# Expert gates of a product-key layer: a table built by adding transfers in main memory, in place of one-hot products on TensorE

## The chip, the cores and the metric

One core of a Trainium2 chip. The metric is the device time of the program in microseconds (us), the median of several executions. The compared kernels run the same inference step on the same inputs.

## What is computed

One decoder layer for 256 prompt tokens and 8 sample tokens (T = 264 columns in all) of width 2048. After the two attention branches comes the part that the change touches, a layer of 16384 experts of which each token takes 16 per head, in 8 heads:

```python
def peer_route(h, w_q, sub_keys):
    q = (h @ w_q).reshape(T, PEER_HEADS, 2, PEER_DK)
    s = jnp.einsum('thpd,hpkd->thpk', q, sub_keys).astype(jnp.float32)
    sv, si = lax.top_k(s, PEER_TOPK)
    cand = (sv[:, :, 0, :, None] + sv[:, :, 1, None, :]).reshape(T, PEER_HEADS, PEER_TOPK * PEER_TOPK)
    cv, ci = lax.top_k(cand, PEER_TOPK)
    ia = jnp.take_along_axis(si[:, :, 0], ci // PEER_TOPK, axis=-1)
    ib = jnp.take_along_axis(si[:, :, 1], ci % PEER_TOPK, axis=-1)
    return ia * N_KEYS + ib, jax.nn.softmax(cv, axis=-1)
...
        act = jax.nn.gelu(jnp.einsum('td,thkd->thk', hi, eu[ii]).astype(jnp.float32), approximate=False)
        return jnp.einsum('thk,thkd->td', (act * gi).astype(hi.dtype), ev[ii])
```

Expert number = 128 ia + ib. Nearly every expert is wanted by some token, so the kernel computes all 16384 x 264 scores densely, takes their gelu, multiplies by a dense table of gates (0 where a token did not choose the expert; the sum of the gates where several heads chose it), and multiplies the result by the dense matrix of expert outputs.

## The kernel before, in words

**Units of weights.** All large products run as "units". A unit is one load of 1 MB (128 x 2048 float32) into a ring of four slots (`RING`, `wr`, issued by SP in `load_w` after `wait_slot`), which ACT rounds to a high part (`high_part`, L420) and DVE completes by a low part (`low_part`, L425), each in four quarters; TensorE then makes three products of every 128 x 128 block (`products`, L577 to L579), 48 matmuls of 264 columns per unit. High and low parts have room for one unit, so a quarter is prepared while TensorE works through the other three quarters of the unit before. Units follow each other in one order (`STREAM`) on SP, ACT, DVE and PE.

**The expert layer** has 128 score units (`peer_u`, one unit for each value of ia: 128 experts) and 128 output units (`peer_v`; four units, a "group", for each four values of ia). The activations of 64 values of ia fill the buffer `ACTS`, so the layer runs in two halves:

1. 64 score units "u0". Between their quarters DVE runs the routing (`routing()`: three passes for 128, 128 and 8 tokens; top-16 of the keys, top-16 of the pairs, softmax), and PE turns the resulting lists so that tokens lie in columns (`turn_results`).
2. `weights(0)`: 66 jobs that make the gates of the first 64 values of ia. For each eight tokens DVE writes two one-hot matrices of the chosen ia (`OHA`, L1928) and ib (`OHB`, L1930), GpSimd multiplies the first by the gates (L1448), PE multiplies them token by token (L1065), and DVE multiplies the activations by the product, read from PSUM (`weigh`, L2083). No unit runs in this stage.
3. A loop `for it in 0..7` that alternates an output group of the first half with four score units of the second half ("vu"), whose activations take the place of those just used.
4. `weights(1)`, as 2.
5. 64 output units ("v1"). In an output group ACT and DVE split the weighted activations (L1341, L2091) and DVE adds the products to x (`add_outputs`, L2101).

Then comes the last normalisation `norm(2)` and the embedding part ("ple"), whose weights `wple` and `pT` GpSimd loads when the expert layer is over (L1456, L1457).

Of the kernel before, what the change touches and what calls it, by code (L numbers as in the profile page):

```python
# [23 lines left out]
P = 128  # L24
# [4 lines left out]
NH = 8  # L29
# [17 lines left out]
STREAM = [("A", 56), ("gates", 32), ("up", 16), ("out", 16), ("wq", 16), ("u0", 64), ("vu", 128), ("v1", 64), ("ple", 16)]  # L47
# [19 lines left out]
for _u in range(32):  # L67
    JOB_LIST += [(f"gate{_u}", 1)] + SLOT.get(_u, [])
JOB_LIST += [("up", 16), ("out", 16),
            ("norm1", 1), ("wq", 16), ("key", 9), ("u0", 64), ("wb0", 66), ("u1", 64), ("wb1", 66), ("norm2", 1), ("ple", 16)]  # L70
JOB = {}
SPLIT_JOBS = ("A", "out", "wq", "u0", "u1", "ple") + tuple(f"gate{_u}" for _u in range(32))
# [15 lines left out]
def stream_of(n):  # L88

    for name, s in (("A", S0["A"]), *((f"gate{u}", S0["gates"] + u) for u in range(32)), ("out", S0["out"]),  # L90
                    ("wq", S0["wq"]), ("u0", S0["u0"]), ("ple", S0["ple"])):
# [11 lines left out]
EXPS, TURN = (19, 43, 51), (28, 52, 56)  # L103
# [5 lines left out]
C_EPS, C_EPS128, C_SEL, C_RT, C_OWNH, C_FOLD, C_END = 1984, 1985, 1986, 2017, 2023, 2027, 2035  # L109


def constants():
# [24 lines left out]
    for half in range(2):  # L137
        for parity in range(2):
            for g in range(4):
                row = 32 * (2 * half + parity) + g  # L140
                c[row, C_OWNH + g] = 1
                c[row, C_FOLD + 4 * half + g] = 1
    c[:, C_EPS] = EPS
# [8 lines left out]
def build(nc, xT, pT, wd, vd, wsmall, wple, subk, kx, vx, lx, state, convst, params, consts, ptab,  # L152
          o_x, o_k, o_v, o_lf, o_sp, o_ss, o_cs):
    with ExitStack() as ctx:
# [100 lines left out]
        ACTS = BIG  # L255
        IDX = CST + C_INV
        assert IDX + 3 * T <= CST + C_CAUS
        OHA = ACTS + HALF * T
        OHB = OHA + 2 * 8 * HALF
        assert OHB + 2 * 8 * P <= NF  # L260

# [19 lines left out]

        FIRST_ON = tuple((a - ACTS) // T for a in (SCORE[0], SCORE[1], RS2))
# [75 lines left out]
        turned, idx_ready, al_ready = sem("turned"), sem("idx_ready"), sem("al_ready")  # L358
# [106 lines left out]
        def _(sp):  # L465
# [71 lines left out]
            loop(S0["u0"], 136, 16)  # L537
            with sp.Fori(0, 16) as it:
                for kind in range(2):
                    for j in range(RING):  # L540
                        s = S0["vu"] + 4 * kind + j
                        wait_slot(sp, it, 8, s, RING)
                        load_w(it, 4, s, (vd, wd)[kind], (j, 200 + j)[kind])
            loop(S0["v1"], 64, 16, vd)
# [15 lines left out]
        def _(pe):  # L560
# [471 lines left out]
            def turn_results(c):  # L1032
                pe.wait_ge(res_ready, c + 1)
                for i in range(3):
                    if c == 2:
                        last = mm(ps[:, 6, i * P:i * P + NS], at(LX + i * P, P, 64), at(ROW_T, NS, 64), start=True, stop=True)
                    else:
                        last = nc.tensor.transpose(ps[:, 4 + c, i * P:(i + 1) * P], at(RES[c] + i * P, P), ident)
                last.then_inc(turned, 1)

            for c in range(3):
                key_scores(c)

            done = 0
            for c in range(4):
                upto = (TURN + (64,))[c] // 4
                with pe.Fori(done, upto) as it:
                    for j in range(RING):
                        split_unit(it, 4, S0["u0"] + j, JOB["u0"] + j)
                done = upto  # L1050
                if c < 3:
                    turn_results(c)

            def weights(half):
                wb = JOB[f"wb{half}"]

                def weights_of(it, j):
                    pe.wait_ge(oha_ready, it * 4 + (33 * half + j + 1))
                    pe.wait_ge(ohb_ready, it * 4 + (33 * half + j + 1))
                    for n in (wb + 2 * j, wb + 2 * j + 1):  # L1060
                        pe.wait_ge(evac[n % 4], it * 2 + n // 4)
                        for i in range(4):
                            t = 4 * (n - wb - 2 * j) + i
                            oha = at(OHA + (j % 2) * 8 * HALF + t * HALF, HALF)
                            last = mm(bank(n)[:, i * P:(i + 1) * P].rearrange("p (r a) -> p r a", a=HALF),  # L1065
                                      at(OHB + (j % 2) * 8 * P + t * P, P),
                                      oha.unsqueeze(1).broadcast_to([P, 2, HALF]), start=True, stop=True)
                        last.then_inc(pe_job, 1)

                with pe.Fori(0, 8) as it:  # L1070
                    for j in range(4):
                        weights_of(it, j)
                weights_of(8, 0)

            def outputs(it, m, s, g, buf):

                pe.wait_ge(al_ready, it * 2 + (g + 1))
                for dq in range(RING):
                    for q in range(RING):
                        pe.wait_ge(y_added, it * 32 + (16 * g + 4 * dq + q + 1))  # L1080
                        wait_low_part(pe, it, m, s + dq, q)
                        for j in range(EG):
                            a = (buf * EG + j) * T
# [5 lines left out]
            weights(0)  # L1089
            pe.wait_ge(idx_ready, 3)  # L1090
            with pe.Fori(0, 8) as it:
                for b in range(2):
                    outputs(it, 16, S0["vu"] + 8 * b, b, b)
                    for j in range(RING):
                        split_unit(it, 16, S0["vu"] + 8 * b + 4 + j, JOB["u1"] + 4 * b + j, 8)
            weights(1)
            with pe.Fori(0, 8) as it:
                for b in range(2):
                    outputs(it, 8, S0["v1"] + 4 * b, 16 + b, b)
# [15 lines left out]
        def _(act):  # L1115
# [190 lines left out]
            def high_only(name):  # L1306

                dense_steps(act, S0[name], 4, high_part, lambda it, j: None)
# [3 lines left out]
            each_block("wq", 4, ACT.Copy, QT, final=False)  # L1312
# [6 lines left out]

            for u in range(64):  # L1320
                for q in range(RING):
                    high_part(act, 0, 0, S0["u0"] + u + 1, q)
                wait_quarter(act, 0, 0, S0["u0"] + u, RING - 1)
                if u in FIRST_ON:
                    act.wait_ge(res_ready, FIRST_ON.index(u) + 1)
                n = JOB["u0"] + u
                A(at(ACTS + u * T, T), bank(n)[:, 0:T], ACT.Gelu).then_inc(evac[n % 4], 1)
                if u in EXPS:
# [3 lines left out]
                    gates = at(RES[c] + 2 * P, 16 * heads, m)  # L1332
                    A(gates, gates, ACT.Exp).then_inc(re_exp, 1)

            def slots(a, n, it, m):
                a = ACTS + a * T
                return at(a + it * m * T, n * T) if isinstance(it, int) else arena[:, bass.ds(it * (m * T) + a, n * T)]

            def high_of_group(it, g, buf):
                rows = at(ACTS, HALF * T).rearrange("p (a t) -> p a t", t=T)[:, bass.ds(it * 8 + 4 * g, EG), :]  # L1340
                A(rd_(AH + buf * EG * T, EG * T).rearrange("p (a t) -> p a t", t=T), rows, ACT.Copy).then_inc(ah_ready, 1)  # L1341

            def value_parts(it, m, s, b, last, nothing_after=False):
                for j in range(RING):
                    for q in range(RING):
                        if not (nothing_after and last and j == RING - 1):
                            high_part(act, it, m, s + j + 1, q)
                    if j == 1 and not (last and b == 1):

                        high_of_group(it, b + 1, 1 - b)  # L1350

            def both(it, last=False):
                for b in range(2):
                    s = S0["vu"] + 8 * b
                    value_parts(it, 16, s, b, last)
                    for j in range(RING):
                        for q in range(RING):
                            high_part(act, it, 16, s + 5 + j, q)
                        wait_quarter(act, it, 16, s + 4 + j, RING - 1)
                        n = JOB["u1"] + 4 * b + j  # L1360
                        if j == 0:
                            act.wait_ge(al_ready, it * 2 + (b + 1))
                        A(slots(4 * b + j, 1, it, 8), bank(n)[:, 0:T], ACT.Gelu).then_inc(evac[n % 4], 1)
# [3 lines left out]
            for half in range(2):  # L1367
                for b in range(4):
                    wait_evac(act, JOB[f"wb{half}"] + 62 + b)
                high_of_group(0, 0, 0)  # L1370
                if half == 0:
                    with act.Fori(0, 7) as it:
# [866 lines left out]
```

## Time and profile before

| | us |
|---|---|
| median of 3 runs | 3101.51 (3099.52 to 3107.52) |
| the profiled execution | 3104.63 |
| its span in the profile | 3103.0 |
| PE busy | 2945.5 (95%) |
| DVE busy | 1918.7 (62%) |
| ACT busy | 1228.9 (40%) |
| POOL (GpSimd) busy | 201.6 (6%) |
| main memory traffic | 519.60 MB, mean 167 GB/s |

The profiled execution took 3.1 us more than the median of the runs; its span is 1.6 us shorter than its own time. Busy times of engines overlap, so the shares tell which engine is never long idle (PE), and the stages have to be looked at one by one to see what each costs.

### The profile page before, as it was taken

To read this page: it belongs to the slowest core of one execution; us is meant where nothing else is said; L and a number is where in the kernel's file an instruction comes from. 1 tells how busy PE (TensorE), PEld (TensorE's weight loads), DVE (VectorE), ACT (ScalarE), POOL (GpSimd) and SP (SyncE) were. 2 spreads that over 40 slices of the span, in tenths; PEclk is the share of its full clock that TensorE was granted. 3 is DMA by queue.
4 is the path that set the end of the run, shared out by engine and by line. 5 is a ranking of instruction groups with operands and counts; after the bars stand their busy time and mean duration, and the time that the engine had idled before them with its cause. 6 is when DMAs were issued, how large, how long until landed. Compare 5 with 4: busy or idle time off the path is not lost.

```text
span 3103.0 us, 60917 instructions
## 1 busy us (share of the span) xinstructions
PE 2945.5 (95%) x23119; PEld 2804.4 (90%) x23119; DVE 1918.7 (62%) x3707; ACT 1228.9 (40%) x2123; POOL 201.6 (6%) x227
## 2 busy tenths in 40 slices
PE   6999999989999998999998799999999978999999
PEld 6999868877878898999997799999999978999989
DVE  4467446545442345588868856656656687777764
ACT  4455421033330244445551144444444412444454
POOL 2100011000000000000004300000000042000000
PEclk8999979989899998999999999999999999999999
DMA  5545335547564444445542154454455512444543
GB/s 189 188 177 180 131 117 188 190 172 297 218 255 164 152 161 153 157 177 179 187 176 82 46 185 176 181 184 176 181 184 176 182 62 73 184 176 178 185 154 123
DMA packets 83934, 519.60 MB, mean 167 GB/s; under 512 B 11170, under 2 KB 11442, under 8 KB 30834
## 3 DMA queue, kind: packets, MB, share of 16 engines
q1 hardware_dynamic: 74882, 488.03, 43.4%
q0 software_dynamic: 7792, 25.95, 2.2%
q10 hardware_dynamic: 1152, 4.19, 0.4%
q8 instruction: 65, 1.06, 0.1%
q14 instruction: 43, 0.35, 0.0%
HBM read 508.75 MB, written 9.39 MB: 167 GB/s over the span
## 4 chain that ended last, share of the span: by engine, by line
PE 90%; DVE 6%; issue 2%; DMA 1%; ACT 0%; DVEq 0%; POOL 0%; POOLq 0%; SPq 0%; ACTq 0%
PE ps L577 25%; PE ps L578 25%; PE ps L579 24%; PE ps L1001 4%; PE ps L811 2%; DVE arena L1930 1%; DVE arena L2083 1%; DVE arena L1928 1%; PE ps L897 1%; PE ps L653 1%; PE ps L637 1%; PE ps L798 1%; PE ps L572 1%; DVE arena L1474 1%; PE ps L934 1%
## 5 line engine op out<-in xcount | busy, mean ns | idle before, releaser
L425 DVE TENSOR_TENSOR split<-arena,split 128x512 fp32r<-128x512 f32 x1568 | 1080.8, 692 | 840.2 <-ACT split L420 833.7
L420 ACT ACTIVATE split<-arena 128x512 fp32r<-128x512 f32 x1568 | 987.5, 631 | 1267.8 <-PE ps L579 1267.3
L577 PE MATMUL ps<-split 128*128 128x264 f32 x4224 | 1216.5, 288 | 45.2 <-DVE split L425 41.5
L578 PE MATMUL ps<-split 128*128 128x264 f32 x4224 | 1206.0, 286 | 0.0
L579 PE MATMUL ps<-split 128*128 128x264 f32 x4224 | 1205.1, 285 | 0.0
L577 PEld LDWEIGHTS ps<-split 128*128 128x128 f32 x4224 | 805.4, 191 | 71.1 <-DVE split L425 35.6
L578 PEld LDWEIGHTS ps<-split 128*128 128x128 f32 x4224 | 806.0, 191 | 0.5
L579 PEld LDWEIGHTS ps<-split 128*128 128x128 f32 x4224 | 801.5, 190 | 0.0
L577 PE MATMUL ps<-rounded,split 128*128 128x264 f32 x2048 | 584.1, 285 | 10.7 <-DVE rounded L2091 10.7
L578 PE MATMUL ps<-rounded,split 128*128 128x264 f32 x2048 | 584.4, 285 | 0.0
L579 PE MATMUL ps<-rounded,split 128*128 128x264 f32 x2048 | 580.6, 283 | 0.0
L577 PEld LDWEIGHTS ps<-rounded,split 128*128 128x128 f32 x2048 | 387.1, 189 | 11.1 <-issue 11.1
L578 PEld LDWEIGHTS ps<-rounded,split 128*128 128x128 f32 x2048 | 386.8, 189 | 0.0
L579 PEld LDWEIGHTS ps<-rounded,split 128*128 128x128 f32 x2048 | 386.3, 189 | 0.0
L2101 DVE TENSOR_TENSOR arena<-arena,ps 128x264 f32<-128x264 f32 x512 | 216.4, 423 | 0.0
L1448 POOL TENSOR_TENSOR arena<-arena 128x512 f32<-128x512 f32 x66 | 122.7, 1860 | 1290.2 <-DVE arena L1928 1290.2
L1065 PE MATMUL ps<-arena 128*128 128x128 f32 x1056 | 134.5, 278 | 47.6 <-POOL arena L1448 47.6
L1065 PEld LDWEIGHTS ps<-arena 128*128 128x128 f32 x1056 | 122.7, 189 | 59.3 <-issue 36.9
L1001 PE MATMUL ps<-arena 128*128 128x264 f32 x512 | 117.2, 391 | 0.7 <-DVE arena L1874 0.7
L1001 PEld LDWEIGHTS ps<-arena 128*128 128x128 f32 x512 | 98.6, 193 | 19.0 <-issue 0.8
L1341 ACT ACTIVATE rounded<-arena 128x1056 fp32r (+1 forms) x32 | 34.3, 1073 | 181.4 <-DVE arena L2083 181.4
L1930 DVE TENSOR_TENSOR arena<-arena 128x1024 f32<-128x1024 f32 x66 | 80.4, 1218 | 0.0
(323 smaller groups left out, 1702.3 us busy)
## 6 DMA issues: line engine op xcount, KB each, us to landing
arena<-in_wd SPq DMA_DIRECT2D x280, 1024.0 KB, 4.8
arena<-in_vd SPq DMA_DIRECT2D x128, 1024.0 KB, 4.8
arena<-in_kx SPq DMA_DIRECT2D x64, 512.0 KB, 4.6
arena<-in_vx SPq DMA_DIRECT2D x32, 512.0 KB, 6.7
arena<-in_vx POOLq DMA_DIRECT2D x32, 512.0 KB, 6.8
early<-in_state SPq DMA_DIRECT2D x8, 512.0 KB, 9.6
o_ss<-early ACTq DMA_DIRECT2D x8, 512.0 KB, 9.1
arena<-in_xT SPq DMA_DIRECT2D x1, 2112.0 KB, 8.6
```

The source lines that it names most:

```text
L420: nc.scalar.activation(ckh(q), at(WR + (s % 4) * D_MODEL + q * QW, QW), ACT.Copy).then_inc(hi_ready, 1)
L425: nc.vector.tensor_tensor(ckl(q), at(WR + (s % 4) * D_MODEL + q * QW, QW), as_f32(ckh(q)), ALU.subtract).then_inc(lo_ready, 1)
L577: mm(out, wh, xh, start=start, stop=False)
L578: mm(out, wh, xl, start=False, stop=False)
L579: return mm(out, wl, xh, start=False, stop=stop)
L811: last = mm(bank(n)[:, i * P:(i + 1) * P], at(lhs + o, P), at(rhs + o, P), start=True, stop=True)
L1001: last = mm(ps[:, n % 4 + 4 * half, 0:T], wr(j)[:, (half * NH + k) * P:(half * NH + k + 1) * P], ot3[:, half * NH + k, :], start=(k == 0), ...
L1065: last = mm(bank(n)[:, i * P:(i + 1) * P].rearrange("p (r a) -> p r a", a=HALF), at(OHB + (j % 2) * 8 * P + t * P, P), oha.unsqueeze(1).br ...
L1341: A(rd_(AH + buf * EG * T, EG * T).rearrange("p (a t) -> p a t", t=T), rows, ACT.Copy).then_inc(ah_ready, 1)
L1448: nc.gpsimd.tensor_tensor(oh, oh, gate, ALU.mult).then_inc(oha_ready, 1)
L1930: V.tensor_tensor(at(OHB + (j % 2) * 8 * P, 8 * P).rearrange("p (t b) -> p t b", b=P), cst(C_IOTA).unsqueeze(1).broadcast_to([P, 8, P]), a ...
L2101: V.tensor_tensor(xt3[:, d, :], xt3[:, d, :], ps[:, 4 + q, 0:T], ALU.add).then_inc(y_added, 1)
```

## The change

The expert layer is no longer halved. The 128 score units run first ("u"), then the 128 output units ("v"). The activations go to a table `acts` in main memory: ACT writes the gelu of a unit to a ring of 16 in the arena (`ACTR`), and SP stores each four of them. The gates are a table `gates` of 128 x 128 x 264 floats in main memory. ACT's queue clears it by 32 transfers during the units "out" and "wq" (`clear_gates`). The routing now ends in element numbers (`LIN`), and GpSimd issues 384 indirect transfers (3 passes x 8 heads x 16 choices), each of which adds one gate of each token to its element of the table; after each 16 it waits until all have landed, since two heads may choose the same expert. For each output group SP loads the group's activations and gates (`load_activations`), GpSimd multiplies them, ACT and DVE split the product. `weights`, `onehots`, `weigh`, `gate_rows` and two of three `turn_results` are gone.

```diff
-STREAM = [("A", 56), ("gates", 32), ("up", 16), ("out", 16), ("wq", 16), ("u0", 64), ("vu", 128), ("v1", 64), ("ple", 16)]
+STREAM = [("A", 56), ("gates", 32), ("up", 16), ("out", 16), ("wq", 16), ("u", 128), ("v", 128), ("ple", 16)]
...
+        gates = nc.dram_tensor("gates", (N_KEYS, P, T), F32, kind="Internal").ap()
+        acts = nc.dram_tensor("acts", (N_KEYS // EG, P, EG * T), F32, kind="Internal").ap()
+        gate_rows = gates.rearrange("a b (t o) -> (a b t) o", o=1)
+        GRP = EG * T
...
+            def store_activations(g):
+                n = JOB["u"] + 4 * g + 3
+                wait_evac(sp, n)
+                sp.dma_start(acts[g], at(ACTR + (g % 4) * GRP, GRP)).then_inc(act_stored, 16)
+
+            def load_activations(g):
+
+                if g >= 2:
+                    sp.wait_ge(al_ready, g - 1)
+                else:
+                    sp.wait_ge(gates_added, 16 * 3 * P)
+                sp.wait_ge(act_stored, 16 * (g + 1))
+                w = gates[4 * g:4 * g + 4].rearrange("a b t -> b a t")
+                sp.dma_start(at(ABUF + g % 2 * GRP, GRP), acts[g]).then_inc(aw_loaded[g % 2], 16)
+                sp.dma_start(at(WBUF + g % 2 * GRP, GRP).rearrange("p (a t) -> p a t", t=T), w).then_inc(aw_loaded[g % 2], 16)
+
+            peel(S0["u"], 136, wd)
+            for g in range(32):
+
+                for j in range(RING):
+                    s = S0["u"] + 4 * (g + 1) + j
+                    wait_slot(sp, 0, 0, s, RING)
+                    load_w(0, 0, s, *((wd, 136 + 4 * (g + 1) + j) if g < 31 else (vd, j)))
+                if g:
+                    store_activations(g - 1)
+            load_activations(0)
+            load_activations(1)
+            store_activations(31)
+            for g in range(32):
+                if g < 31:
+                    for j in range(RING):
+                        s = S0["v"] + 4 * (g + 1) + j
+                        wait_slot(sp, 0, 0, s, RING)
+                        load_w(0, 0, s, vd, 4 * (g + 1) + j)
+                if g < 30:
+                    load_activations(g + 2)
...
-            weights(0)
-            pe.wait_ge(idx_ready, 3)
-            with pe.Fori(0, 8) as it:
+            pe.wait_ge(rows_read, 1)
+            with pe.Fori(0, 16) as it:
                 for b in range(2):
-                    outputs(it, 16, S0["vu"] + 8 * b, b, b)
-                    for j in range(RING):
-                        split_unit(it, 16, S0["vu"] + 8 * b + 4 + j, JOB["u1"] + 4 * b + j, 8)
-            weights(1)
-            with pe.Fori(0, 8) as it:
-                for b in range(2):
-                    outputs(it, 8, S0["v1"] + 4 * b, 16 + b, b)
+                    outputs(it, b)
...
+            def clear_gates(it, a):
+
+                dst = gates.rearrange("(g a) b t -> g b a t", a=EG)
+                dst = dst[it * 4 + a // 4] if isinstance(it, int) else dst[bass.ds(it * 4 + a // 4, 1)].rearrange("o b a t -> (o b) a t")
+                act.dma_start(dst, at(ZT, T).unsqueeze(1).broadcast_to([P, EG, T])).then_inc(gates_zero, 16)
...
+            def high_of_group(it, b):
+                act.wait_ge(prod_ready, it * 2 + (b + 1))
+                A(rd_(AH + b * GRP, GRP), at(ABUF + b * GRP, GRP), ACT.Copy).then_inc(ah_ready, 1)
...
-            for half in range(2):
-                def gate_rows(it, j):
-                    pool.wait_ge(oh_step, it * 4 + (33 * half + j + 1))
-                    oh = at(OHA + (j % 2) * 8 * HALF, 8 * HALF).rearrange("p (t a) -> p t a", a=HALF)
-                    gate = arena[:, bass.ds(it * 32 + (IDX + 2 * T + 8 * j), 8)].unsqueeze(2).broadcast_to([P, 8, HALF])
-                    nc.gpsimd.tensor_tensor(oh, oh, gate, ALU.mult).then_inc(oha_ready, 1)
...
-            pool.wait_ge(y_added, 516)
+            pool.wait_ge(gates_zero, 16 * N_KEYS // EG)
+            for c in range(3):
+                pool.wait_ge(lin_ready, c + 1)
+                m = P if c < 2 else NS
+                source = RES[c] + 2 * P if c < 2 else RT2 + 2 * P
+                for h in range(NH):
+                    for k in range(16):
+                        e = 16 * h + k
+                        pool.indirect_dma_start(gate_rows, bass.IndirectOffsetOnAxis(at(LIN + c * P + e, 1, m).bitcast(U32), 0),
+                                                at(source + e, 1, m), None, compute_op=ALU.add).then_inc(gates_added, 16)
+                    pool.wait_ge(gates_added, 16 * (P * c + 16 * h + 16))
+
             pool.dma_start(at(WPL, PLE_KT * D_MODEL), wple).then_inc(ple_in, 16)
             pool.dma_start(at(PTI, PLE_KT * T), pT).then_inc(ple_in, 16)
+
+            with pool.Fori(0, 16) as it:
+                for b in range(2):
+                    pool.wait_ge(aw_loaded[b], it * 32 + 32)
+                    a = at(ABUF + b * GRP, GRP)
+                    nc.gpsimd.tensor_tensor(a, a, at(WBUF + b * GRP, GRP), ALU.mult).then_inc(prod_ready, 1)
...
+                    m2, firsts = (m, RE) if c < 2 else (NS, RT2)
+                    row = at(LT, P, m2)
+                    ch(V.tensor_scalar(row, at(firsts, P, m2), float(P * T), cst(C_TOK + c, 1, m2), ALU.mult, ALU.add))
+                    ch(V.scalar_tensor_tensor(out=row, in0=at(firsts + P, P, m2), scalar=float(T), in1=row, op0=ALU.mult, op1=ALU.add))
+                    V.tensor_copy(at(LIN + c * P, P, m2).bitcast(U32), row).then_inc(lin_ready, 1)
```

What the queues hold now, at two places. On GpSimd, behind the load of the sub-keys (`SK`), the kernel before has the multiplications of the one-hot rows and then the loads for "ple":

```order
L1450 ISA
L1448 ISA [waits onehot_step]
L1448 TENSOR_TENSOR arena<-arena 128x512
L1445 REGISTER_ALU
...
L1450 COMPARE_AND_BRANCH
L1448 TENSOR_TENSOR arena<-arena 128x512 [waits onehot_step]
L1456 DMA arena<-in_wple 128x4096 [waits y_added]
L1457 DMA arena<-in_pT 128x528
```

and the changed kernel (L1442 is the adding transfer, L1453 the product of activations and gates; the pair of L1442 rows stands 24 times in all):

```order
L1442 DMA gates<-arena 4325376x1 [waits lin_ready,gates_zero]
L1442 DMA gates<-arena 4325376x1 x15
...
L1442 DMA gates<-arena 4325376x1 [waits gates_added]
L1442 DMA gates<-arena 4325376x1 x15
L1446 DMA arena<-in_wple 128x4096 [waits gates_added]
L1447 DMA arena<-in_pT 128x528
...
L1453 TENSOR_TENSOR arena<-arena 128x1056 [waits aw_loaded0]
L1453 TENSOR_TENSOR arena<-arena 128x1056 [waits aw_loaded1]
```

All 384 adding transfers now stand on GpSimd's queue ahead of the products. On SP, where score units end and output units begin, the changed kernel has (L483 the loads of units, L549 a store of activations, L559 and L560 the loads of a group's activations and gates):

```order
L483 DMA arena<-in_vd 128x2048 [waits lo_ready] x4
L549 DMA acts<-arena 128x1056 [waits evac3]
L559 DMA arena<-acts 128x1056 [waits act_stored,gates_added]
L560 DMA arena<-gates 128x4x264
L559 DMA arena<-acts 128x1056 [waits act_stored,gates_added]
L560 DMA arena<-gates 128x4x264
L549 DMA acts<-arena 128x1056 [waits evac3]
L483 DMA arena<-in_vd 128x2048 [waits lo_ready] x4
L559 DMA arena<-acts 128x1056 [waits act_stored,al_ready]
L560 DMA arena<-gates 128x4x264
```

Before, SP had nothing but loads of units there. The first loads of activations and gates now stand behind the loads of the first four output units, and wait for the last adding transfer.

## Rows read from the trace of the kernel before

**Rows 1.** The page: engines, and the chain that ended last.

```profile
PE 2945.5 (95%) x23119; PEld 2804.4 (90%) x23119; DVE 1918.7 (62%) x3707; ACT 1228.9 (40%) x2123; POOL 201.6 (6%) x227
PE 90%; DVE 6%; issue 2%; DMA 1%; ACT 0%; DVEq 0%; POOL 0%; POOLq 0%; SPq 0%; ACTq 0%
```

**Rows 2.** Windows by stage: u0, weights(0), vu, weights(1), v1.

```profile
core 0: us, PE busy (x) PEld busy (x) DVE busy (x) ACT busy (x) POOL busy (x), PEclk, DMA share, GB/s
1284.00:1656.00 372.00, 372.00 (x3078) 371.80 (x3077) 293.30 (x776) 188.11 (x329) 3.68 (x2) 1.00 0.49 177
1656.00:1756.00 100.00, 68.98 (x541) 62.95 (x540) 96.52 (x135) 2.36 (x4) 61.36 (x33) 0.98 0.04 15
1756.00:2501.00 745.00, 745.00 (x6142) 745.00 (x6141) 456.51 (x782) 353.44 (x589) 0.00 (x0) 1.00 0.50 179
2501.00:2596.00 95.00, 67.74 (x532) 61.74 (x532) 91.00 (x131) 1.99 (x3) 57.70 (x31) 0.99 0.03 11
```

**Rows 3.** Timeline of PE where stages meet (start, duration, instruction).

```profile
1284.04 0.39 PE L577 MATMUL ps<-split 128*128 128x264 f32 x1
...
1656.87 0.28 PE L579 MATMUL ps<-split 128*128 128x264 f32 x1
...
1755.29 0.58 PE L577 MATMUL ps<-rounded,split 128*128 128x264 f32 x1 [7.22 <-DVE rounded L2091]
...
2501.06 0.28 PE L579 MATMUL ps<-split 128*128 128x264 f32 x1
...
2595.69 0.58 PE L577 MATMUL ps<-rounded,split 128*128 128x264 f32 x1 [3.46 <-DVE rounded L2091]
```

**Rows 4.** Timeline of ACT and DVE in an output group of v1.

```profile
2701.92 0.63 ACT L420 ACTIVATE split<-arena 128x512 fp32r<-128x512 f32 x1 [0.82 <-PE ps L579]
...
2703.91 1.07 ACT L1341 ACTIVATE rounded<-arena 128x1056 fp32r x1
...
2702.59 0.69 DVE L425 TENSOR_TENSOR split<-arena,split 128x512 fp32r<-128x512 f32 x1 [0.42 <-ACT split L420]
2703.20 0.42 DVE L2101 TENSOR_TENSOR arena<-arena,ps 128x264 f32<-128x264 f32 x1
...
2705.14 1.26 DVE L2091 TENSOR_TENSOR rounded<-arena,rounded 128x1056 fp32r<-128x1056 f32 x1
```

**Rows 5.** Timeline of PE after the expert layer.

```profile
2983.65 1.16 PE L1108 MATMUL ps<-arena 128*128 128x264 f32 x4 [1.60 <-DMA arena<-in_pT]
```

**Rows 6.** Timeline of DVE: the last steps of the routing's passes.

```profile
1420.84 0.29 DVE L2030 TENSOR_TENSOR arena<-arena 128x128 f32<-128x128 f32 x1
...
1557.48 0.29 DVE L2030 TENSOR_TENSOR arena<-arena 128x128 f32<-128x128 f32 x1
...
1598.12 0.68 DVE L2038 TENSOR_TENSOR arena<-arena 64x128 f32<-64x128 f32 x3
```

**Rows 7.** Instructions of POOL by line and shape: transfers issued, products.

```profile
L1448 POOL TENSOR_TENSOR arena<-arena 128x512 f32<-128x512 f32 x66 | 122.7, 1860 | 1290.2 <-DVE arena L1928 1290.2
L1394 POOL DMA_DIRECT2D early<-in_lx x64 | 31.2, 488 | 26.5 <-issue 26.5
L451 POOL DMA_DIRECT2D arena<-in_vx x32 | 17.0, 530 | 272.2 <-PE ps L897 238.8 <-issue 33.4
L1402 POOL DMA_DIRECT2D o_lf<-arena x1 | 1.0, 1036 | 0.0
```

**Rows 8.** DMA issues: KB each, median us from issue to landing.

```profile
arena<-in_kx SPq DMA_DIRECT2D x64, 512.0 KB, 4.6
early<-in_lx POOLq DMA_DIRECT2D x64, 4.0 KB, 2.9
o_lf<-arena POOLq DMA_DIRECT2D x1, 12.0 KB, 7.0
```

**Rows 9.** Timeline where DVE and POOL collide, end of weights(0).

```profile
1749.51 1.84 POOL L1448 TENSOR_TENSOR arena<-arena 128x512 f32<-128x512 f32 x1 [3.55 <-DVE arena L1928]
...
1750.37 1.53 DVE L1928 TENSOR_TENSOR arena<-arena 128x512 f32<-128x512 f32 x1
```

More of the change, by code:

```diff
@@ L69 @@
 JOB_LIST += [("up", 16), ("out", 16),
-            ("norm1", 1), ("wq", 16), ("key", 9), ("u0", 64), ("wb0", 66), ("u1", 64), ("wb1", 66), ("norm2", 1), ("ple", 16)]
+            ("norm1", 1), ("wq", 16), ("key", 9), ("u", 128), ("norm2", 1), ("ple", 16)]
 JOB = {}
-SPLIT_JOBS = ("A", "out", "wq", "u0", "u1", "ple") + tuple(f"gate{_u}" for _u in range(32))
+SPLIT_JOBS = ("A", "out", "wq", "u", "ple") + tuple(f"gate{_u}" for _u in range(32))
 PJ = []
@@ L1075, in outputs @@
-            def outputs(it, m, s, g, buf):
-                pe.wait_ge(al_ready, it * 2 + (g + 1))
+            with pe.Fori(0, TURN // 4) as it:
+                for j in range(RING):
+                    split_unit(it, 4, S0["u"] + j, JOB["u"] + j)
+            pe.wait_ge(res_ready, 1)
+            for i in range(3):
+                last = mm(ps[0:NS, 6, i * P:(i + 1) * P], at(ROW_T, NS, 64), at(LX + i * P, P, 64), start=True, stop=True)
+            last.then_inc(turned, 1)
+            with pe.Fori(TURN // 4, 32) as it:
+                for j in range(RING):
+                    split_unit(it, 4, S0["u"] + j, JOB["u"] + j)
@@ L1343, in value_parts @@
[L1343 to L1352, printed above, removed]
+                    rows = at(RES[c] + 2 * P, 16 * heads, m)
@@ L1353, in both, with value_parts @@
+                    A(rows, rows, ACT.Exp).then_inc(re_exp, 1)
+            with act.Fori(4, 8) as it:
+                for u in range(16):
+                    gelu(it, u)
+            def high_of_group(it, b):
+                act.wait_ge(prod_ready, it * 2 + (b + 1))
+                A(rd_(AH + b * GRP, GRP), at(ABUF + b * GRP, GRP), ACT.Copy).then_inc(ah_ready, 1)
+            def value_parts(it, last=False):
                 for b in range(2):
-                    s = S0["vu"] + 8 * b
-                    value_parts(it, 16, s, b, last)
@@ L1365, in _ @@
+                        if j == 1 and not (last and b == 1):
+                            high_of_group(it, b + 1) if b == 0 else high_of_group(it + 1, 0)
             for j in range(4):
                 act.wait_ge(state_saved[j], 32)
-            for half in range(2):
[L1368 to L1372, printed above, removed]
-                        both(it)
-                    both(7, True)
-                else:
-                    with act.Fori(0, 7) as it:
-                        for b in range(2):
-                            value_parts(it, 8, S0["v1"] + 4 * b, b, False)
-                    for b in range(2):
-                        value_parts(7, 8, S0["v1"] + 4 * b, b, True)
+            high_of_group(0, 0)
@@ L1382, in _ @@
+            with act.Fori(0, 15) as it:
+                value_parts(it)
+            value_parts(15, True)
             norm(2)
@@ L2137, in _ @@
+            low_of_group(0, 0)
+            with dve.Fori(0, 15) as it:
+                add_outputs(it)
+            add_outputs(15, True)
             dve.wait_ge(y_added, 516)
```

228 lines of the change are left out of this document (65 added, 163 removed).

## The prediction

> **What bounds the kernel now.** I read the page first, then a table of windows with one row for each stage of the expert layer, then PE's timeline at the seams, then the queues of GpSimd. The page says that PE is busy 95% of the span and that 90% of the chain that ended last is PE's [rows 1]; the reader should see that only a stage without PE work, or a wait of PE, can be worth anything. The windows show where such a stage is. In u0 and vu PE is busy every microsecond (372.00 of 372, 745.00 of 745) at full clock, and DMA engines are busy half the time. In weights(0) and weights(1) DVE is the full one (96.5 of 100, 91.0 of 95), PE has 68 us of small products, and DMA is almost idle, 0.04 and 0.03 [rows 2]. So two stages of the expert layer are bound by DVE and build only the gate table.
>
> PE's timeline gives their exact price. The last product of u0 starts at 1656.87 and the first of vu at 1755.29: 98.4 us. The same pair around weights(1) is 2501.06 and 2595.69: 94.6 us. Together 193.0 us [rows 3]. It also gives the pace of a unit: u0 is 64 units from 1284.04 to 1656.99, 5.83 us each, and vu is 128 units in 745 us, 5.82 us each. Score units and output units cost the same, and mixing them is free.
>
> **What is removed.** Both weight stages, 193.0 us of PE's time line, all of it on the path. The 256 units stay: 256 x 5.83 us whichever way they are ordered, so the reordering costs nothing. The ends of the stages (7.2 us and 3.5 us of PE's wait for DVE's first low part of activations [rows 3]) lie inside the 193.0. The two dropped turns of results are six small products, below 1 us; I take 0.
>
> **What is added at the one seam that is left.** In the changed order SP issues the first loads of activations and gates only behind the fourth output unit's load, which waits for the low part of the last score unit. That low part comes 1.4 us after a quarter of PE ends (ACT 0.63, DVE 0.69, and 0.1 of hops [rows 4]), one unit ahead, so 5.83 - 1.4 = 4.4 us before PE ends its score units. A 512 KB load lands 4.6 us after its issue [rows 8]; here a unit of 1 MB and a store stand in front of two such loads, and I take 6.5 us (bounds 4.6 and 3 x 4.6 = 13.8). Then GpSimd's product of 1056 elements, ACT's 1.07 and DVE's 1.26 [rows 4] follow in series. GpSimd took 1.86 us for 512 elements [rows 7]. But of that 1.84 us at 1749.51 it stood beside a DVE instruction until about 1750.4 and ended at 1751.35 [rows 9], which leaves 0.95 us for 512, or 2.0 us for 1056; the upper bound is 1.86 x 1056 / 512 = 3.8. Sum: -4.4 + 6.5 + 2.0 + 1.07 + 1.26 + 0.5 for hops = 7 us of PE idle (bounds 5 and 16). I take 7.
>
> **What becomes cheaper at the end.** `wple` and `pT` are loaded before the output units, so PE's wait of 1.60 us for `pT` [rows 5] goes: 1.6 us.
>
> **The output units with GpSimd beside them.** DVE's L1928 took 1.53 us in place of 0.69 where it met a GpSimd product [rows 9]: an instruction of DVE that reads two tensors of SBUF waits until GpSimd is done. Every group gets one product of 2.0 to 3.8 us, so one low part of the group may come that much late. A low part is ready 1.4 us after its quarter ends and is needed three quarters later, 3 x 1.46 = 4.4 us: 3.0 us of slack, which hides 2.0 us whole. At 3.8 us the excess is 0.8 us, with the add behind it (0.42) 1.2 us, 32 times: 39 us. DVE has the time, since four units need 16 x (0.61 + 0.42) + 1.26 = 18 us (0.61 is L425 less the overlap with what follows it, 2703.20 - 2702.59 [rows 4]) and a group lasts 23.3 us. I take 0; bounds 0 and 39.
>
> **Transfers that hide.** The table of gates and the activations are 17.3 MB each, written and read once: 69 MB more. A unit is 1 MB in 5.83 us at a DMA share of 0.49 [rows 2]. Clearing adds 0.54 MB to each of 32 units, the stores and loads 0.14 and 0.27 MB to each later one. Even at half the efficiency, because the rows are 1056 bytes, the share stays under 0.8; the ring of four units covers 17 us of delay. Cost 0; if that cover went, units of "out" and "wq" would wait. The instruction to issue one is within ACT's 0.82 us of idle time in every quarter [rows 4].
>
> **The adding transfers, the term that decides.** The trace has none, so they are bounded. They start when a pass of the routing ends: pass 0 at 1421, pass 1 at 1558 [rows 6], pass 2 after the turn behind unit 56, 1284.0 + 57 x 5.83 = 1616. Three small DVE instructions for the element numbers follow each, 1 us. They must all have landed when SP comes to the first load, at 1284.0 + 128 x 5.83 - 4.4 = 2026. Call r the time of one transfer of 128 tokens, with its share of the wait after each 16.
>
> - Lower bound: GpSimd issues a plain transfer of 128 partitions in 0.53 us [rows 7] and a small one lands in 2.9 us [rows 8]: r = 0.53 + 2.9 / 16 = 0.71.
> - Upper bound: nothing overlaps and each lasts as long as a small one takes to land: r = 2.9. Were it the 7.0 us of `o_lf` [rows 8], r = 7.0; but that transfer was queued behind 2 MB of others, so I use 7.0 only for the wait after 16.
> - Nearest row: `o_lf` writes 384 pieces of 32 bytes from 128 partitions to main memory, the only scattered small store here. GpSimd took 1.04 us to issue it [rows 7]. r = 1.04 + 7.0 / 16 = 1.48. I take this. Pass 2 has only 8 tokens, so the one-row loads are nearest, 0.49 us each with 26.5 / 64 = 0.41 us between them [rows 7], and 2.9 / 16 = 0.18: 1.07 us.
>
> With 1.48: pass 0 is 128 x 1.48 = 189 us, to 1611; pass 1 to 1801; pass 2 adds 137, to 1938. That is 88 us before 2026, so nothing waits. In general the end is 1422 + 256 r + 137, so r may grow to (2026 - 1422 - 137) / 256 = 1.82 before PE waits.
>
> Here a rule bears. `o_lf`'s row shows 1.04 us of issue, and the 64 loads of `in_lx` follow each other every 0.89 us though each lands only after 2.9: transfers of one queue overlap. The Trainium skill, DMA: Bandwidth & Descriptors, in its anatomy of a transfer issued by GpSimd, gives about 2.0 us fixed for each, mostly the receipt of the last write. If that were the pace, all 384 would end at 1422 + 768 = 2190, 164 us late; by the rows' overlap it is paid once in 16.
>
> **Sum.** 3104.6 - 193.0 + 7 - 1.6 = 2917 for the profiled execution; against the median, 3.1 us lower, 2914 us.
>
> **Rivals.**
>
> *A. Late, but still ahead.* r between 1.82 and 2.55: PE waits 256 (r - 1.82), so at r = 2.2 the time is 2914 + 97 = 3011. For it: the offsets are read from SBUF by GpSimd, while DVE runs L425 for 0.69 us in each 1.46; a meeting like that in [rows 9] could add some tenths to each issue. The Trainium skill, SBUF — State Buffer, in the section on who interferes with whom, says that such a DVE instruction holds off a GpSimd read, and that one of two SBUF inputs does not hold the writing of descriptors; the rows show the first for products only. Against it: 0.34 us each are needed even to reach the edge.
>
> *B. The adding transfer is slow: slower than before.* Each must read its destination, add and write it back, 128 places of 4 bytes, on engines that are half busy with 1 MB loads. If one takes the 2.9 us that a small load takes to land and the next doesn't overlap it, the passes 0 and 1 last 256 x 2.9 = 742 us, the end is 1422 + 742 + 137 = 2301, 275 us after 2026, and the time is 2914 + 275 = 3189. If pass 2 pays 2.9 too: 1422 + 384 x 2.9 = 2536, and 3424. It is decided at r = 2.55, where 256 (r - 1.82) = 187. The place is SP's wait for `gates_added` before the first load of activations; PE would stand idle there once. For it: no row shows a read-modify-write, and eight places per DMA engine could cost 0.3 us each. Against it: the overlap of `in_lx`.
>
> *C. The seam and the collisions of DVE and GpSimd at their bounds.* 9 us and 39 us more: 2962. DVE's slack speaks against it.
>
> *D. The table is never a saving, since PE would lose the same elsewhere.* It would need units slower than 5.83 us; with DMA at half load I see no cause, and give it no chance of its own.
>
> **How the numbers follow.** About 0.3% (9 us) is what a measurement of this kernel can tell from no change. The forecast, 2914, has 0.55, C 0.04, A 0.12, a time within 9 us of before 0.02, and B 0.27. So faster 0.71, same 0.02, slower 0.27. The skill's 2.0 us per transfer for all 384 would give 2914 + 164 = 3078 and lies in A's part. The range must reach into B, which holds more than two in ten: low 2900 (the seam at its lower bound, loads hidden a little better), high 3330 (r = 3.45 for passes 0 and 1), which leaves about one in ten above. The likeliest case's own range is 2900 to 2935.
>
> **What would show it.** Right: no L1065, L1928, L1930; 128 score units in 746 us at full clock; the last adding transfer lands before the score units end, near 1940; one idle stretch of PE of 5 to 16 us between "u" and "v"; output units at 5.83 us with no wait for DVE. Issue times near 1.0 us in POOL's rows confirm 1.48. Wrong: one long idle stretch of PE behind the score units, with SP waiting for GpSimd's transfers; its length over 256 gives r - 1.82. C would show as a wait of PE for L425 once in each group, and L425's mean above 0.69 us.

## The result, and the profile after

| | before | changed |
|---|---|---|
| median of 7 runs, us | 3106.0 (3099.52 to 3109.87) | 3118.15 (3116.4 to 3121.26) |
| the profiled execution, us | 3104.63 | 3116.4 |
| its span, us | 3103.0 | 3114.7 |

The ratio is 1.0041, with a 95% interval of 1.003 to 1.0053: the changed kernel is slower by 0.4%. The forecast was 2914 us. The two weight stages are gone, as forecast, and a wait of nearly the same length has come.

The page of the changed kernel: busy times, slices, the chain that ended last, and two groups of instructions. They answer to [rows 1].

```profile
PE 2809.4 (90%) x22057; PEld 2682.6 (86%) x22057; DVE 1784.3 (57%) x3451; ACT 1229.0 (39%) x2123; POOL 753.0 (24%) x577
PE   6999999989999998999999999900399999999989
POOL 2100011000000000005776777777410011010000
PE 69%; POOL 18%; issue 5%; DMA 4%; DVE 3%; ACT 0%; SPq 0%; DVEq 0%; POOLq 0%; ACTq 0%
L1442 POOL DMA_INDIRECT gates<-arena x384 | 594.4, 1548 | 441.1 <-DVE arena L2042 246.0 <-issue 126.4 <-DMA gates<-arena 68.8
L1453 POOL TENSOR_TENSOR arena<-arena 128x1056 f32<-128x1056 f32 x32 | 79.7, 2489 | 644.2 <-DMA arena<-gates 644.2
```

PE's slices show two zeros where there were none, and POOL's row shows what ran there: the 384 adding transfers (L1442). GpSimd, 0% of the chain before, is 18% of it now; PE fell from 90% to 69%. The waits say who waited for whom (us in total, times, longest):

```profile
PE ps L614 <- DVE rounded L2067: 204.4, 1, 204.4
DVE rounded L2067 <- ACT rounded L1353: 199.8, 1, 199.8
ACT rounded L1353 <- POOL arena L1453: 199.1, 1, 199.1
POOL gates L1442 <- issue: 126.4, 360, 4.6
POOL gates L1442 <- DMA gates<-arena: 68.8, 23, 6.2
...
SPq L559 <- DMA gates<-arena: 190.0, 1, 190.0
```

Read it from below: SP's first load of activations (L559) waits 190.0 us for the last adding transfer to land; GpSimd's product waits for that load, ACT for the product, DVE for ACT, and PE for DVE, once, 204.4 us. PE's timeline gives the account of the span. These are, in the changed kernel, the last product of the score units, the first and the last of the output units, and then the last of the output units in the kernel before:

```profile
2028.79 0.28 PE L616 MATMUL ps<-split 128*128 128x264 f32 x1
2233.48 0.58 PE L614 MATMUL ps<-rounded,split 128*128 128x264 f32 x1 [204.41 <-DVE rounded L2067]
2981.42 0.28 PE L616 MATMUL ps<-rounded,split 128*128 128x264 f32 x1
```

```profile
2971.32 0.28 PE L579 MATMUL ps<-rounded,split 128*128 128x264 f32 x1
```

From start to start the one gap is 204.7 us, in place of 98.4 + 94.6: +11.6. The first score unit starts 1.4 us later (1285.45 against 1284.04). The 256 units together take 743.34 + 747.94 = 1491.3 us in place of 1494.2: -2.9. From the last output product to the end of the span it is 133.3 us in place of 131.7: +1.6. The sum is +11.7, as measured (3114.7 - 3103.0).

Windows of the changed kernel, in the columns of [rows 2]: score units beside the transfers, the idle stretch, output units.

```profile
1560.00:1700.00 140.00, 140.00 (x1160) 139.55 (x1159) 77.09 (x151) 69.90 (x124) 100.62 (x62) 1.00 0.74 204
...
2032.00:2213.00 181.00, 0.00 (x0) 0.00 (x0) 0.00 (x0) 0.00 (x0) 140.09 (x105) 0.50 0.05 0
2213.00:2233.00 20.00, 0.00 (x0) 0.00 (x0) 2.79 (x1) 1.08 (x1) 7.37 (x5) 0.50 0.82 306
2234.00:2982.00 748.00, 747.70 (x6144) 747.49 (x6142) 609.14 (x1053) 350.06 (x543) 74.84 (x30) 1.00 0.61 222
```

The score units lose nothing to the transfers beside them, though the DMA share is 0.74 where it was 0.49. In the idle stretch nothing runs but GpSimd; its transfers there move almost no bytes (0 GB/s, share 0.05). That already speaks for a cost per instruction. The output units run at 748 / 128 = 5.84 us, where they took 5.82 before.

### The profile page after: what moved, and what is told of

Read it like the earlier page. It is cut to its first block, busy times and chain, and to the rows that moved or that the text cites. A ratio compares the mean times of both kernels' runs of the same rounds, so it can differ in the third digit from the quotient of the medians.

```text
span 3114.7 us, 57711 instructions
## 1 busy us (share of the span) xinstructions
PE 2809.4 (90%) x22057; PEld 2682.6 (86%) x22057; DVE 1784.3 (57%) x3451; ACT 1229.0 (39%) x2123; POOL 753.0 (24%) x577
## 4 chain that ended last, share of the span: by engine, by line
PE 69%; POOL 18%; issue 5%; DMA 4%; DVE 3%; ACT 0%; SPq 0%; DVEq 0%; POOLq 0%; ACTq 0%
PE ps L614 18%; PE ps L615 18%; PE ps L616 18%; POOL gates L1442 18%; PE ps L1038 4%; DMA gates<-arena 3%; PE ps L848 2%; PE ps L934 1%; PE ps L690 1%; PE ps L674 1%; PE ps L609 1%; PE ps L835 1%; DVE arena L1470 1%; PE ps L971 1%; PE ps L666 1%
## 5 line engine op out<-in xcount | busy, mean ns | idle before, releaser
L433 DVE TENSOR_TENSOR split<-arena,split 128x512 fp32r<-128x512 f32 x1568 | 1137.4, 728 | 796.1 <-ACT split L428 785.0
L614 PE MATMUL ps<-rounded,split 128*128 128x264 f32 x2048 | 583.0, 285 | 204.4 <-DVE rounded L2067 204.4
L1442 POOL DMA_INDIRECT gates<-arena x384 | 594.4, 1548 | 441.1 <-DVE arena L2042 246.0
L1453 POOL TENSOR_TENSOR arena<-arena 128x1056 f32<-128x1056 f32 x32 | 79.7, 2489 | 644.2 <-DMA arena<-gates 644.2
L2067 DVE TENSOR_TENSOR rounded<-arena,rounded 128x1056 fp32r<-128x1056 f32 x32 | 42.0, 1314 | 199.8 <-ACT rounded L1353 199.8
L1038 PEld LDWEIGHTS ps<-arena 128*128 128x128 f32 x512 | 97.9, 191 | 18.7 <-issue 0.8
L1353 ACT ACTIVATE rounded<-arena 128x1056 fp32r<-128x1056 f32 x32 | 34.3, 1072 | 199.1 <-POOL arena L1453 199.1
L459 POOL DMA_DIRECT2D arena<-in_vx x32 | 17.0, 531 | 277.1 <-PE ps L934 249.8
```

Of the source, the lines that this page charges most:

```text
L433: nc.vector.tensor_tensor(ckl(q), at(WR + (s % 4) * D_MODEL + q * QW, QW), as_f32(ckh(q)), ALU.subtract).then_inc(lo_ready, 1)
L614: mm(out, wh, xh, start=start, stop=False)
L1038: last = mm(ps[:, n % 4 + 4 * half, 0:T], wr(j)[:, (half * NH + k) * P:(half * NH + k + 1) * P], ot3[:, half * NH + k, :], start=(k == 0), ...
L1353: A(rd_(AH + b * GRP, GRP), at(ABUF + b * GRP, GRP), ACT.Copy).then_inc(ah_ready, 1)
L1442: pool.indirect_dma_start(gate_rows, bass.IndirectOffsetOnAxis(at(LIN + c * P + e, 1, m).bitcast(U32), 0), at(source + e, 1, m), None, com ...
L1453: nc.gpsimd.tensor_tensor(a, a, at(WBUF + b * GRP, GRP), ALU.mult).then_inc(prod_ready, 1)
```

## The experiments

Two theories stood after the comparison. **Fixed cost:** each adding transfer occupies GpSimd for a time that hardly depends on how many rows it carries, so 384 instructions are the price. **Contention:** the adding in main memory, beside loads on the same DMA engines, or the meetings with DVE at SBUF, stretches each transfer.

**E1, without the transfers.** The loop that issues them is left out, and SP waits in their place:

```diff
-                    sp.wait_ge(gates_added, 16 * 3 * P)
+                    sp.wait_ge(lin_ready, 3)
+                    sp.wait_ge(gates_zero, 16 * N_KEYS // EG)
```

> Leaves out all 384 adding transfers, so the gate table stays zero and the expert layer adds nothing; everything else of the change stays, SP waits for the clearing and the element numbers in their place. Every theory: the wait of 190.0 us of SP for the transfers goes. What is left of PE's gap of 204.4 us between score and output units is the seam alone, forecast at 7 us (5 to 16), so 2917 to 2928 us. If the time stays above 2960, something else of the change (activations through main memory, clearing, products on GpSimd) costs too, and the forecast's other terms were wrong as well.

Measured: 2922.82 us (one run). Everything else of the change together costs nothing beyond the seam, which is 12.4 us and not 7 (the wait of PE in E1's profile, in the same columns):

```profile
PE ps L615 <- DVE rounded L2062: 12.4, 1, 12.4
```

**E2, without pass 2.**

```diff
-                for h in range(NH):
+                for h in range(NH if c < 2 else 0):
```

with SP's wait lowered to `16 * 2 * P`.

> Leaves out the 128 transfers of pass 2 (8 sample tokens, 1/33 of the gates); passes 0 and 1 stay. In the changed kernel these 256 end at about 1992 us, before SP comes to the first load at 2026, and pass 2 fills 1992 to 2215. Fixed cost for each instruction, paid one to one once SP waits: 2917 to 2928 us. If bytes or places decided (pass 2 moves 1024 of 33792 gates), leaving it out would give back only 3% of 790 us, 24 us: 3092.

Measured: 2921.94 us, ratio 0.9408 (0.9392 to 0.9424). Taking away 3% of the gates gives back 196 us. So the lateness was worth its full length, and pass 2, which moves almost nothing, was the part that made it late. Its 256 transfers:

```profile
L1442 POOL DMA_INDIRECT gates<-arena x256: 1548/1551/2217, 1421.2 to 1988.8; - x128
...
  issue: 87.8, 240
  DMA gates<-arena: 60.2, 15
```

(durations in ns, minimum/median/maximum, then first and last start). The last starts at 1988.8, ahead of SP's first load at 2022.0 (timeline below).

**E3, eight rows in every transfer.**

```diff
-                m = P if c < 2 else NS
+                m = NS
```

> All 384 transfers stay, but those of passes 0 and 1 carry 8 tokens in place of 128 (the gates of the other tokens are left out). Fixed cost theory: each still takes 1.33 us of GpSimd and 0.30 us before the next, about 0.1 for meetings with DVE, and 1.5 to 2.5 us after 16: 1.87 us each, the last lands near 2140, the time is 3030 us (3010 to 3050). Theory that the DMA engines' read-modify-write of 128 places sets the pace: 1/16 of the places, all done before 2026, 2921 us, and the issue of one takes well under 1 us.

Measured: 3034.09 us (one run), 4 us from the expectation of the fixed cost theory and 113 us from the other. Sixteen times fewer places in two thirds of the transfers save 14% of a transfer's time on GpSimd:

```profile
L1442 POOL DMA_INDIRECT gates<-arena x384: 1333/1336/2297, 1417.6 to 2137.9; - x192
```

The median falls from 1551 ns (128 rows, E2) to 1336 ns (8 rows): 215 ns for 120 rows, 1.8 ns a row, over a fixed 1.32 us. The pause of 0.30 us between two instructions stays.

**E4, the transfers after the score units.** GpSimd first waits for the last score unit:

```diff
             pool.wait_ge(gates_zero, 16 * N_KEYS // EG)
+            wait_done(pool, JOB["u"] + 127)
```

> GpSimd starts the 384 transfers only when PE has ended its score units (near 2029 us), so no weight loads and no DVE instructions run beside them. Fixed cost theory: 256 x (1.55 + 0.30) + 16 waits of about 3 us + 223 for pass 2 = 745 us, the last lands near 2775, the time is 3675 us (3640 to 3710). Theory of contention with DVE for the port or with loads for the DMA engines: without both a transfer of 128 takes under 1.3 us with its pause, the time is under 3530. The wait after 16 transfers tells the share of the loads: 5.5 us if it is the landing itself, under 3 if it was the queue behind 1 MB loads.

Measured: 3656.18 us (one run), 19 us below the fixed cost expectation and far above the contention one. With PE, DVE, ACT and the loads silent (busy 0.00 us and 0 GB/s from 2030 to 2500), a transfer of 128 rows still takes 1.55 us, and the next starts 0.30 us later (timeline):

```profile
2054.21 1.55 POOL L1443 DMA_INDIRECT gates<-arena  x1 [0.30 <-issue]
2056.06 1.55 POOL L1443 DMA_INDIRECT gates<-arena  x1 [0.30 <-issue]
2059.33 1.55 POOL L1443 DMA_INDIRECT gates<-arena  x1 [1.72 <-DMA gates<-arena]
```

So contention is not what the price consists of, but it adds to it. From the first transfer's start to the last one's it is 724.2 us here and 788.3 in the changed kernel: 64 us, a third of the 190.0 that SP waits. At one to one the changed kernel without them would take 3118 - 64 = 3054 us (an estimate), faster than before. For passes 0 and 1 it is 505.8 us here against 567: 25 of the 61 are longer transfers, 29 longer waits for landing, the rest pauses. The wait after 16 transfers is 1.7 us here (the expectation's 3 was too high, which is the larger part of the 19 us: 16 x 1.3 = 21), and 57.0 / 16 = 3.6 us in the changed kernel's passes 0 and 1, where 1 MB loads and DVE run beside; no run separates the two. The meetings with DVE show in the changed kernel's own timeline:

```profile
1860.44 1.79 POOL L1442 DMA_INDIRECT gates<-arena  x1 [0.31 <-issue]
1862.53 1.55 POOL L1442 DMA_INDIRECT gates<-arena  x1 [0.30 <-issue]
1864.38 1.55 POOL L1442 DMA_INDIRECT gates<-arena  x1 [0.30 <-issue]
1866.24 1.79 POOL L1442 DMA_INDIRECT gates<-arena  x1 [0.31 <-issue]
...
1860.11 0.69 DVE L433 TENSOR_TENSOR split<-arena,split 128x512 fp32r<-128x512 f32 x1 [0.75 <-ACT split L428]
1863.01 0.69 DVE L433 TENSOR_TENSOR split<-arena,split 128x512 fp32r<-128x512 f32 x1 [0.75 <-ACT split L428]
1865.91 0.69 DVE L433 TENSOR_TENSOR split<-arena,split 128x512 fp32r<-128x512 f32 x1 [0.75 <-ACT split L428]
```

A transfer that starts while DVE is in a low part (1860.44 inside 1860.11 to 1860.80, 1866.24 inside 1865.91 to 1866.60) takes 0.24 us longer; one that has a low part in its middle (1862.53, with 1863.01) does not. That fits a read of the offsets at the start, but only the times are shown, not the cause. The mean over passes 0 and 1 is 421.3 / 256 = 1.65 us (E2's busy time), so meetings cost 0.10 us of 2.21 us. The Trainium skill, SBUF — State Buffer, section "Who interferes with whom", says that a DVE instruction with two SBUF inputs contends with a GpSimd instruction that reads SBUF. The 0.24 us at the start of a transfer agree with it.

**F1, pass 2 in eight transfers.** PE now turns the sample tokens' lists so that 128 rows are 8 tokens x 16 choices, with a column for each head. A head's transfer still names each place once:

```diff
-                last = mm(ps[0:NS, 6, i * P:(i + 1) * P], at(ROW_T, NS, 64), at(LX + i * P, P, 64), start=True, stop=True)
+                last = mm(ps[:, 6, i * NH:(i + 1) * NH], at(LX + i * P, P, 64), at(ROW_H, NH, 64), start=True, stop=True)
...
+            for c in range(2):
+                pool.wait_ge(lin_ready, c + 1)
+                for h in range(NH):
+                    for k in range(16):
+                        add(c, 16 * h + k, gates_added)
+                    if c == 1:
+                        pool.wait_ge(lin_ready, 3)
+                        add(2, h, gates_added)
+                    pool.wait_ge(gates_added, 16 * (16 * h + 16 if c == 0 else P + 17 * (h + 1)))
```

> Computes the whole layer. The sample tokens' gates are laid out as 128 rows (8 tokens x 16 choices) with a column for each head, so pass 2 takes 8 transfers of 128 rows in place of 128 transfers of 8, each issued behind a head of pass 1 and covered by that head's wait. Fixed cost theory: 120 instructions fewer, the last transfer lands near 1992 + 8 x 1.95 = 2008 us, before SP comes at about 2022, and the time is that of the runs without pass 2, 2922 us (2917 to 2928). If the number of places moved decided, nothing would change: 3118 us.

Measured: 2925.19 us, ratio 0.9425 (0.941 to 0.944). The whole layer is computed, all gates are moved, and 120 instructions fewer are worth 193 us. The last transfer starts at 2010.4:

```profile
L1438 POOL DMA_INDIRECT gates<-arena x264: 1549/1552/2089, 1417.5 to 2010.4; - x132
```

The cover is thin. The last transfer has landed at 2016.9, and SP issues its first load of activations at 2018.3. PE's wait at the seam is 18.0 us here and not 12.4:

```profile
PE ps L615 <- DVE rounded L2072: 18.0, 1, 18.0
```

GpSimd's loads for "ple" (2.3 MB) are issued at 2016.9, just ahead of SP's, and the product starts 14.8 us after SP's first load, where in E2, with those loads issued at 1992.4, it is 9.3. That they stand in front is likely the cause; no run tests it alone.

**F2, two semaphores.** The heads go in the order 0, 1, 2, 3 of pass 0, then pass 1 and pass 0 in turn, and each waits for its own pass only.

```diff
+            for c, h in [(0, 0), (0, 1), (0, 2), (0, 3), (1, 0), (0, 4), (1, 1), (0, 5), (1, 2), (0, 6), (1, 3), (0, 7),
+                         (1, 4), (1, 5), (1, 6), (1, 7)]:
+                if h == 0:
+                    pool.wait_ge(lin_ready, c + 1)
+                else:
+                    pool.wait_ge((gates_added, added1)[c], 16 * (16, 17)[c] * h)
```

> f1, and the heads of passes 0 and 1 alternate from the fifth head on, each pass with its own semaphore, so that a head waits for the head before it of its own pass while the other pass's 16 transfers are issued. The landing of 5.5 us after each head is hidden for about ten of 16 heads: the last transfer lands 45 to 65 us earlier than in f1, near 1950. Since SP comes only at 2022, the time stays that of f1 within 4 us; if it falls by 40 us, SP was still waiting in f1 and my account of the cover is wrong.

Measured: 2922.78 us, ratio 0.9408 (0.9393 to 0.9423), so the time stays within 4 us of F1, as expected. But the last transfer starts at 1989.2, not near 1950, and that part of the expectation is a miss:

```profile
L1440 POOL DMA_INDIRECT gates<-arena x264: 1549/1552/2218, 1426.8 to 1989.2; - x132
...
  DVE arena L2053: 273.6, 2
  issue: 81.7, 256
  DMA gates<-arena: 21.4, 6
```

The waits for landing fell from 60.8 us (F1) to 21.4. The first line has a second wait now, 27.5 us beyond the 246.1 of F1, and it stands at one place (timelines of GpSimd and DVE):

```profile
1595.39 1.55 POOL L1440 DMA_INDIRECT gates<-arena  x1 [0.31 <-issue]
1624.41 1.97 POOL L1440 DMA_INDIRECT gates<-arena  x1 [27.47 <-DVE arena L2053]
```

```profile
1623.96 0.17 DVE L2053 CAST arena<-arena 128x8 uint32<-128x8 f32 x1
```

The transfer at 1624.41 is the 81st: behind four heads of pass 0 and the first of pass 1 (80 transfers) comes the first of the sample tokens, and their element numbers are written only at 1623.96. Pass 1 itself did not wait: its first transfer started 0.30 us after the one before it. From first to last start the chain is 562.4 us, against 592.9 in F1; without the 27.5 it would be 535 (an estimate), 58 shorter than F1's, within the 45 to 65 that were expected. The sample tokens' first transfer behind a later head would have avoided the wait; no run does that.

**F3, earlier loads.** F2, with `load_activations(0)` and `load_activations(1)` ahead of the last four loads of units:

```diff
             for g in range(32):
+                if g == 31:
+                    load_activations(0)
+                    load_activations(1)
...
-            load_activations(0)
-            load_activations(1)
             store_activations(31)
```

> f2, and SP issues the first two groups' loads of activations and gates ahead of the last four loads of units, so that GpSimd's first two products are done before PE ends its score units. The seam of 12.4 us shrinks to ACT's and DVE's work on the first group, 0.3 + 0.6 + 0.4 + 1.1 + 1.3 = 3.7 us and hops, about 4: 2913 us (2909 to 2919), 6.2% below the kernel before. If the seam is bound by something else it stays at 12 and the time at 2922.

Measured: 2912.07 us (2909.39 to 2914.25), ratio 0.9377 (0.9364 to 0.939): 6.2% below the kernel before, and faster than both kernels. The seam, in E2 and then in F3 (timelines; start, duration, instruction):

```profile
2022.00 0.37 SPq L559 DMA_DIRECT2D arena<-acts  x1
2031.29 2.41 POOL L1453 TENSOR_TENSOR arena<-arena 128x1056 f32<-128x1056 f32 x1 [37.73 <-DMA arena<-gates]
2033.81 1.08 ACT L1353 ACTIVATE rounded<-arena 128x1056 fp32r<-128x1056 f32 x1 [7.40 <-POOL arena L1453]
2034.17 2.41 POOL L1453 TENSOR_TENSOR arena<-arena 128x1056 f32<-128x1056 f32 x1 [0.47 <-DMA arena<-gates]
2034.93 2.76 DVE L2067 TENSOR_TENSOR rounded<-arena,rounded 128x1056 fp32r<-128x1056 f32 x1 [8.07 <-ACT rounded L1353]
2037.93 0.58 PE L614 MATMUL ps<-rounded,split 128*128 128x264 f32 x1 [12.46 <-DVE rounded L2067]
```

```profile
2001.42 0.36 SPq L562 DMA_DIRECT2D arena<-acts  x1
...
2031.52 0.58 PE L617 MATMUL ps<-rounded,split 128*128 128x264 f32 x1 [3.44 <-DVE rounded L2078]
```

In E2 the loads take 9.3 us from the first issue to the product, and DVE's low part takes 2.76 us in place of 1.26 because GpSimd is in its second product. In F3 the load is issued 20 us earlier, and PE waits 3.4 us.

## Why the prediction was wrong, point by point

- **What is removed, 193.0 us: right.** E1's span is 2921.1 against 3103.0, 181.9 us less; 193.0 - 12.4 for the seam would be 180.6. The rest is small: the 256 units take 2.4 us less in E1, the part before them 0.8 less, and the part behind them 1.6 more. So the units kept their pace in both orders.
- **Transfers that hide, cost 0: right.** The DMA share in the score units rose to 0.74 and PE stayed fully busy.
- **Output units with GpSimd beside them, 0 (bound 39): right.** The collisions are there: a low part at 2308.87 took 2.57 us beside a product. The slack of 3.0 us covered them, for PE's only wait there is the one at the start.
- **The end, -1.6 us: the wait went, the saving did not come.** PE no longer waits for `pT`, but the part behind the last output product is 133.3 us in place of 131.7. The 32 products of the last normalisation take 8.99 us in place of 7.40, with a granted clock of 0.50 from 2986 to 2988 where it was 1.00 in all of them before, and PE then waits 3.3 us for DVE's first low part of "ple" where it waited 1.4:

```profile
PE ps L577 <- DVE split L1478: 1.8, 3, 1.4
PE ps L614 <- DVE split L1474: 3.7, 3, 3.3
```

  Why the clock fell there stays open.
- **The seam, 7 us (bounds 5 and 16): mis-sized, 12.4.** In E2 SP came 3.5 us before PE ended and not 4.4; the loads needed 9.3 us and not 6.5; GpSimd's product 2.41 and not 2.0; and DVE's meeting with the second product, 1.5 us, was not in the sum.
- **The adding transfers: here it failed.** The place was right, SP's wait for `gates_added`, with PE idle once; so was the edge: SP came to it at 2215.6 - 190.0 = 2025.6, forecast 2026. The term "Nearest row: `o_lf`", r = 1.48, was too small, and so was pass 2; the bounds, 0.71 and 2.9, held. Passes 0 and 1 ran from 1424.8 to 1991.7, 567 us or 2.21 us each:

| part of r, passes 0 and 1 | forecast | measured |
|---|---|---|
| on GpSimd | 1.04 | 1.65 |
| pause before the next | 0 | 88.6 / 256 = 0.35 |
| share of the wait after 16 | 0.44 | 57.0 / 256 = 0.22 |
| sum | 1.48 | 2.22 |

  The pause was a plain omission: [rows 7] had it, 0.41 us between the loads of `in_lx`, and the forecast used it for pass 2 alone. With it r would have been 1.89, already past the edge of 1.82.
- **Pass 2: the worse slip for a reader to learn from.** It was costed as one-row loads, 1.07 us each, 137 us. It took 1.33 us on GpSimd, 0.30 us of pause and its waits: from 1991.7 to the landing at 2215, 224 us, or 1.75 us each. The ends add up: 567 - 379 = 188 us too short in passes 0 and 1, 87 in pass 2, and 3 for the later start, less 88 of margin, are 190 us late, against 190.0 measured.
- **The rivals.** A had the mechanism (late, PE waits one to one) and, at r = 2.2, the right r; it gave 3011 because it kept pass 2 at 137 us. B was named for read-modify-write at 2.9 us each. Its outcome came true, barely, but not its mechanism: E3 and E4 show that places and memory are not what takes most of the time. The Trainium skill, DMA: Bandwidth & Descriptors, section "Anatomy of one DMA — SWDGE (gpsimd) path", gives a fixed cost of about 2.0 us for each transfer issued by GpSimd, mostly the receipt. Used as the pace, that would have put the end at 2190, and the last transfer landed at 2215. The pace is near, but the cause is not that one. The landing overlaps: in E4 a transfer of 128 rows lands 3.0 us after its issue, and the next one starts after 1.85. What does not overlap is the issue.
- **Chances.** The range, 2900 to 3330, held the time; the 0.71 for faster did not come true, and the distance of r = 1.48 from the edge of 1.82 was smaller than the unknown in a kind of instruction that no row showed.

## What to carry to other kernels

The indirect transfers on GpSimd were paid by the instruction, not by the byte: 1.63 us with eight rows and 1.85 us with 128, pause included. Count them and fill their rows first. A serial chain of them hides under other work only as long as that work lasts, so work out when it starts, how long it runs and who waits for its last one. A pass over a few leftover items deserves the same count as the large ones: here 3% of the data was 28% of the chain, and laying it out differently was worth 193 us. And look at when each link's input is ready: in F2 one transfer put too early in the order held up the chain for 27 us.

## What the runs showed of the hardware that was not expected

- An adding indirect transfer costs GpSimd 1.33 us with 8 rows and 1.55 us with 128, the same with all other engines silent, and the next one starts 0.30 us later.
- Scattered additions of 4 bytes in main memory kept up with this rate beside 1 MB loads: the wait for sixteen of them to land was 1.7 us with the loads silent and 3.6 us on average beside them. One of 128 rows lands 3.0 us after its issue with the loads silent (E4).
- In the stretch shown, a transfer of 128 rows that starts inside a DVE instruction with two SBUF inputs takes 0.24 us longer.
- A GpSimd product of 1056 elements takes 2.41 us, where 512 elements had been recorded at 1.86 us with a DVE instruction beside them [rows 9]: the recorded time held the other engine's.
